# The first two weight units of a decoder layer worked on side by side, their weights in three pieces each

## The reference

```python
def _half_ffn(x, norm_g, w_gate, w_up, w_down):
    h = _rmsnorm(x, norm_g)
    return x + 0.5 * ((jax.nn.silu(h @ w_gate) * (h @ w_up)) @ w_down)

xp = _half_ffn(xp, ffn1_norm, ffn1_w_gate, ffn1_w_up, ffn1_w_down)     # D_FF = 2816
u, q, k, v = _project(_rmsnorm(xp, mix_norm), pos_p, w_in, q_norm, k_norm)
mixed = concatenate([_pool_mix(u, ...), _swa_prompt(q, k, v, sinks)])
xp = xp + mixed @ w_out
xp = _half_ffn(xp, ffn2_norm, ffn2_w_gate, ffn2_w_up, ffn2_w_down)
```

## Time and profile before

| | us |
|---|---|
| median of three runs | 880.23 |
| lowest and highest of them | 879.80, 883.03 |
| the profiled execution, whole | 880.45 |
| its span (first to last instruction) | 878.4 |
| TensorE busy in the span | 871.3 |
| VectorE, ScalarE busy | 660.3, 394.0 |

### The profile page before, as it was taken

How to read it: one execution, slowest core, us unless ns; L and a number is a source line. 1 busy time by engine, 2 the same in 40 slices (tenths; PEclk the granted TensorE clock), 3 DMA queues, 4 the chain that set the end, 5 groups by cost and what they waited for, 6 DMA issues and landing times.

```text
span 878.4 us, 17072 instructions
## 1 busy us (share of the span) xinstructions
PE 871.3 (99%) x7088; PEld 856.9 (98%) x7088; DVE 660.3 (75%) x979; ACT 394.0 (45%) x639; POOL 32.4 (4%) x37
## 2 busy tenths in 40 slices
PE   8999999999999999999999999999999999999998
PEld 7999999999999999999888999999999999999998
DVE  6979647997569986754887697996479975799754
ACT  7635313554224553443754465554125542255420
POOL 0000000000000000012423000000000000000000
PEclk9999999999999999999999999999999999999999
DMA  7333323332424322522321415324233324334241
GB/s 251 117 121 114 133 66 121 121 121 84 145 65 164 121 76 84 190 76 60 113 65 60 145 38 169 120 76 175 75 121 120 121 85 145 111 122 128 85 121 61
DMA packets 43180, 98.57 MB, mean 112 GB/s; under 512 B 4288, under 2 KB 5056, under 8 KB 43104
## 3 DMA queue, kind: packets, MB, share of 16 engines
q1 hardware_dynamic: 41376, 95.01, 33.6%
q10 hardware_dynamic: 1728, 2.48, 0.8%
HBM read 93.53 MB, written 3.60 MB: 111 GB/s over the span
## 4 chain that ended last, share of the span: by engine, by line
PE 96%; DVE 2%; DMA 1%; issue 1%; ACT 0%; SPq 0%; DVEq 0%; ACTq 0%
PE ps L612 44%; PE ps L740 15%; PE ps L742 15%; PE ps L741 15%; PE ps L642 1%; PE ps L978 1%; PE ps L969 1%; DMA xT<-x 1%; PE ps L960 1%; PE ps L799 1%; PE ps L933 0%; PE ps L883 0%; PE ps L657 0%; DVE wlo L1522 0%; DVE hlo L1649 0%
## 5 line engine op out<-in xcount | busy, mean ns | idle before, releaser
L740 PE MATMUL ps<-xhi,whi 128*128 128x260 f32 (+1 forms) x1092 | 310.2, 284 | 0.1
L742 PE MATMUL ps<-xhi,wlo 128*128 128x260 f32 (+1 forms) x1092 | 310.0, 284 | 0.0
L741 PE MATMUL ps<-xlo,whi 128*128 128x260 f32 (+1 forms) x1092 | 309.6, 284 | 0.0
L740 PEld LDWEIGHTS ps<-xhi,whi 128*128 128x128 f32 x1092 | 205.4, 188 | 0.8 <-issue 0.6
L742 PEld LDWEIGHTS ps<-xhi,wlo 128*128 128x128 f32 x1092 | 205.5, 188 | 0.0
L741 PEld LDWEIGHTS ps<-xlo,whi 128*128 128x128 f32 x1092 | 205.4, 188 | 0.0
L1593 DVE TENSOR_TENSOR wlo<-full,whi 128x1024 fp32r<-128x1024 f32 (+1 forms) x117 | 160.3, 1394 | 0.0
L1118 ACT CAST whi<-raw 128x1024 fp32r<-128x1024 f32 (+1 forms) x75 | 75.2, 1003 | 154.9 <-PE ps L612 147.9
L612 PE MATMUL ps<-hhi,whi 128*128 128x268 f32 (+1 forms) x690 | 140.4, 285 | 0.3
L612 PE MATMUL ps<-hlo,whi 128*128 128x268 f32 (+1 forms) x690 | 140.1, 284 | 0.0
L612 PE MATMUL ps<-hhi,wlo 128*128 128x268 f32 (+1 forms) x690 | 139.8, 284 | 0.0
(11 more groups left out here) (194 smaller groups left out, 1070.4 us busy)
## 6 DMA issues: line engine op xcount, KB each, us to landing
full<-gu SPq DMA_DIRECT2D x78, 512.0 KB, 4.4
raw<-d SPq DMA_DIRECT2D x32, 448.0 KB, 3.5
full<-gu SPq DMA_DIRECT2D x39, 256.0 KB, 2.7
raw<-d SPq DMA_DIRECT2D x16, 512.0 KB, 3.7
raw<-w_in SPq DMA_DIRECT2D x10, 512.0 KB, 3.7
raw<-gu SPq DMA_DIRECT2D x9, 512.0 KB, 4.3
raw<-w_out SPq DMA_DIRECT2D x8, 512.0 KB, 4.3
xT<-x SPq DMA_DIRECT2D x8, 268.0 KB, 5.8
```

The source lines that it names most:

```text
L740: nc.tensor.matmul(dst, whi_t, xhi_t, start=(first and pr == 0), stop=False, skip_group_check=True)
L741: nc.tensor.matmul(dst, whi_t, xlo_t, start=False, stop=False, skip_group_check=True)
L742: last = nc.tensor.matmul(dst, wlo_t, xhi_t, start=False, stop=(pr == KC - 1), skip_group_check=True)
```

## The change

- `WARM` goes from 6 to 5.
- The weights of units 0 and 1 come in three pieces each, `PIECES` = tiles 0 and 1, tiles 2 and 3, tiles 4 to 7. `BEFORE_X` gives ahead of which chunk of x (by its place in `ORDER`) a piece is loaded and split: piece 0 of unit 0 ahead of the first chunk, piece 0 of unit 1 ahead of the second, piece 1 of both ahead of the third, piece 2 of both ahead of the fifth. SP, ScalarE and VectorE all follow it.
- TensorE works both units in one loop over the chunks, `first_two`: for each chunk, x high with `whi` and `wlo` of unit 0 and of unit 1, and then x low of the chunk before with `whi` of both. The number of matmuls is the same. `unit_done` is counted up for unit 0 and for unit 1 at the last step.
- `whi_ready` and `wlo_ready` are counted up at the third piece of a unit; the first two pieces have `first_hi` and `first_lo`.
- What follows unit 1 on each engine is as before.

```diff
--- before.py
+++ after.py
@@ -110,8 +110,10 @@
 
 NORM_AT = (1, 2, 6)
 SQSUM_AT = (0, KD - 1, 2 * (KD - 1))
-WARM = 6
-FIRST = 2
+WARM = 5
+PIECES = ((0, 2), (2, 4), (4, 8))
+
+BEFORE_X = {0: ((0, 0),), 1: ((1, 0),), 2: ((0, 1), (1, 1)), 4: ((0, 2), (1, 2))}
 ORDER = (0, 2, 4, 6, 1, 3, 5, 7)
 
 
@@ -295,7 +297,7 @@
     x_loaded = [sem(f"x_loaded{k}") for k in range(KD)]
     fixed_loaded = sem("fixed_loaded")
     gains_loaded = sem("gains_loaded")
-    first_loaded = sem("first_loaded")
+    piece_loaded = [[sem(f"piece_loaded{c}{j}") for j in range(2)] for c in range(2)]
     first_hi = sem("first_hi")
     first_lo = sem("first_lo")
     mixin_loaded = sem("mixin_loaded")
@@ -518,14 +520,16 @@
                 if d == 3 and p < 2:
                     load_unit(s, p + 1, 0)
 
-        sp.dma_start(raw[:, 0, 0:FIRST, :].rearrange("p t c -> p (t c)"), a["gu1"][:, 0:FIRST * P]
-                     ).then_inc(first_loaded, 16)
-        for k in ORDER:
+        def load_piece(c, j):
+            lo, hi = PIECES[j]
+            sp.dma_start(raw[:, c, lo:hi, :].rearrange("p t c -> p (t c)"), a["gu1"][:, (c * KD + lo) * P:(c * KD + hi) * P]
+                         ).then_inc(raw_loaded[c] if j == 2 else piece_loaded[c][j], 16)
+
+        for t, k in enumerate(ORDER):
+            for c, j in BEFORE_X.get(t, ()):
+                load_piece(c, j)
             sp.dma_start(xT[:, k, :], a["x"][:, k, :]).then_inc(x_loaded[k], 16)
-            if k == ORDER[FIRST - 1]:
-                sp.dma_start(raw[:, 0, FIRST:KD, :].rearrange("p t c -> p (t c)"), a["gu1"][:, FIRST * P:KD * P]
-                             ).then_inc(raw_loaded[0], 16)
-        for u in range(1, 2 * PLAIN[0]):
+        for u in range(2, 2 * PLAIN[0]):
             load_plain(0, u)
             if u == 5:
                 load_unit(0, 0, 0)
@@ -632,18 +636,31 @@
             for _ in range(WARM):
                 nc.tensor.matmul(nsum[:, 0, 0:2 * P], hid[:, 0:P], hid[:, 0:2 * P], start=True, stop=True)
 
-        def early(c, dst, pairs, n, wait, first=False, last=False):
+        def first_two(n):
 
             x = x_split(n)
-            for t, k in enumerate(ORDER):
-                for i, (w, lo) in enumerate(pairs):
-                    wait(t, i)
-                    for h in range(2):
-                        done = nc.tensor.matmul(dst[:, h, 0:n], w[:, c % 2, t, :], x(k, lo, h),
-                                                start=(first and t == 0 and i == 0),
-                                                stop=(last and t == KD - 1 and i == len(pairs) - 1))
-            if last:
-                done.then_inc(unit_done, 1)
+            for t in range(KD + 1):
+                for c in range(2):
+                    if t == KD:
+                        break
+                    if c == 0:
+                        pe.wait_ge(xhi_ready, t + 1)
+                    for i, w in enumerate((whi, wlo)):
+                        if t in (0, 2):
+                            pe.wait_ge(first_lo if i else first_hi, t + c + 1)
+                        elif t == 4:
+                            pe.wait_ge(wlo_ready if i else whi_ready, c + 1)
+                        for h in range(2):
+                            nc.tensor.matmul(pair[c][:, h, 0:n], w[:, c, t, :], x(ORDER[t], 0, h),
+                                             start=(t == 0 and i == 0), stop=False)
+                if t:
+                    pe.wait_ge(xlo_ready, t)
+                    for c in range(2):
+                        for h in range(2):
+                            done = nc.tensor.matmul(pair[c][:, h, 0:n], whi[:, c, t - 1, :], x(ORDER[t - 1], 1, h),
+                                                    start=False, stop=(t == KD))
+                        if t == KD:
+                            done.then_inc(unit_done, 1)
 
         def norm_sums(i, c0, n):
 
@@ -668,33 +685,11 @@
...
             warm_up()
-            early(0, pair[0], [(whi, 0), (wlo, 0)], n, hi_there, first=True)
-            early(0, pair[0], [(whi, 1)], n, lo_there, last=True)
-            early(1, pair[1], [(whi, 0), (whi, 1)], n, hi_1, first=True)
-            early(1, pair[1], [(wlo, 0)], n, lo_1, last=True)
+            first_two(n)
             plain(2, turn, [0, 1])
             norm_sums(0, 0, n)
             plain(2, turn, [2, 3])
@@ -1305,16 +1300,20 @@
 
         act.wait_ge(consts_made, 2)
         nc.scalar.copy(warm[:, :], eps[:, :]).then_inc(warmed, 1)
-        act.wait_ge(first_loaded, 16)
-        nc.scalar.copy(whi[:, 0, 0:FIRST, :], raw[:, 0, 0:FIRST, :]).then_inc(first_hi, 1)
-        act.wait_ge(gains_loaded, 16)
-        for k in ORDER:
+
+        def piece_hi(c, j):
+
+            lo, hi = PIECES[j]
+            act.wait_ge(raw_loaded[c] if j == 2 else piece_loaded[c][j], 16)
+            nc.scalar.copy(whi[:, c, lo:hi, :], raw[:, c, lo:hi, :]).then_inc(whi_ready if j == 2 else first_hi, 1)
+
+        for t, k in enumerate(ORDER):
+            for c, j in BEFORE_X.get(t, ()):
+                piece_hi(c, j)
+            if t == 0:
+                act.wait_ge(gains_loaded, 16)
             act.wait_ge(x_loaded[k], 16)
             x_hi(x_pair(xhi7, k, NH_ALL), k, 0, 0, NH_ALL)
-            if k == ORDER[FIRST - 1]:
-                act.wait_ge(raw_loaded[0], 16)
-                nc.scalar.copy(whi[:, 0, FIRST:KD, :], raw[:, 0, FIRST:KD, :]).then_inc(whi_ready, 1)
-        split_hi(1)
         for k in range(KD):
             nc.scalar.activation(sqx[:, k, :], xT[:, k, :], ACT.Square).then_inc(sqx_ready, 1)
             if k == 3:
@@ -1762,22 +1761,22 @@
                     if d:
                         add_square(1, d, 0, NH_ALL)
 
-        def first_weights_lo(hi_there, tiles):
-
-            dve.wait_ge(hi_there, 1)
-            return nc.vector.tensor_tensor(wlo[:, 0, tiles, :], raw[:, 0, tiles, :], whi[:, 0, tiles, :].bitcast(F32),
-                                           ALU.subtract)
-
-        first_weights_lo(first_hi, slice(0, FIRST)).then_inc(first_lo, 1)
-        dve.wait_ge(gains_loaded, 16)
+        def piece_lo(c, j):
+
+            lo, hi = PIECES[j]
+            dve.wait_ge(whi_ready if j == 2 else first_hi, c + 1 if j == 2 else 2 * j + c + 1)
+            nc.vector.tensor_tensor(wlo[:, c, lo:hi, :], raw[:, c, lo:hi, :], whi[:, c, lo:hi, :].bitcast(F32),
+                                    ALU.subtract).then_inc(wlo_ready if j == 2 else first_lo, 1)
+
         for t, k in enumerate(ORDER):
+            for c, j in BEFORE_X.get(t, ()):
+                piece_lo(c, j)
+            if t == 0:
+                dve.wait_ge(gains_loaded, 16)
             x_lo(x_pair(xlo7, k, NH_ALL), x_pair(xhi7, k, NH_ALL), t, k, 0, 0, NH_ALL)
-            if t == FIRST - 1:
-                first_weights_lo(whi_ready, slice(FIRST, KD)).then_inc(wlo_ready, 1)
         dve.wait_ge(fixed_loaded, 16)
         nc.vector.tensor_scalar(nsink[:, :], fixed[:, C_SINK:C_IDENT], -1.0, None, ALU.mult)
         nc.vector.tensor_scalar(ngain[:, :], gains[:, 0:3 * KD], -1.0, None, ALU.mult).then_inc(ngain_made, 1)
-        split_lo(1)
 
         for k in range(1, KD):
             dve.wait_ge(sqx_ready, k + 1)
```

More of the change, by code:

```diff
@@ L669, in plain_products_1 @@
             n = NH_ALL
[L671 to L688, removed]
             def plain(c, dst, ks=None):
```

## The result

| | before | changed |
|---|---|---|
| median of the executions timed side by side, us | 882.9 | 887.69 |
| lowest and highest of them | 879.8, 883.49 | 886.19, 889.27 |
| profiled execution, whole and span | 880.45, 878.4 | 886.19, 884.1 |
| its mean granted clock | 1.000 | 0.994 |

The ratio is 1.0065, 95% interval 1.005 to 1.008: slower by 0.65%, 4.8 us between the two medians, where 0.26% was forecast as the likeliest and 885.2 was the upper end of the range. The two profiled executions are 5.7 us of span apart.

What follows compares the result with a forecast made beforehand. TensorE was taken as the bound, 96% of the span; the profiled 880.45 plus 2.3 us of lag gave 882.75, and 882.6 with the median 0.2 lower. The range was 880.6 to 885.2.

Steps and rivals of the forecast that it cites:

- The supply and E: Opening, units 0 and 1: chunks and casts keep up, TensorE waits last for the third chunk until 8.8, finishing at 18.2.
- E: Time at which TensorE finishes the first two units: 18.2 us, floor 17.4, 19.1 with slow small pieces.
- The release of unit 0's place: Unit 2's cast must wait until unit 0 is finished; TensorE idles 3.6 us and resumes at 21.8, 1.05 later than before.
- lag: How much later TensorE runs than in the kernel before: 2.3 us at the spread, kept to the end; 1.5 to 3.2.
- The clock: TensorE's granted clock in the new 3.6 us hole: the forecast counted no fall to half pace.
- a rival with 0.18 of the chance: TensorE's clock falls in the new hole, half pace from 21.8 to 27.1: lag 3.4 to 4.5, 884.0 to 884.9; chance 0.18.
- Matmuls close on both sides: Reason for giving the clock's fall less chance: the long hole has matmuls close before and after it.
- the 5.3 us of the start: Work TensorE needed at kernel start before reaching the upper clock level, taken as the length of half pace behind the hole.
- The base: Starting time of the sum: profiled execution 880.45 us, median of three runs 880.23.
- the same: Forecast outcome, on the slow side: 0.26% slower, under the 0.5% a measurement can tell from no change; chance 0.87.

Runs made afterwards that it cites:

- e1: Changed kernel with a place of its own for unit 2's high and low parts, so their making waits for no unit: 881.55 us, ratio to before 0.9997.
- e2: Kernel before with one edit, the cast of unit 2 waits until both first units are finished: 889.72 us, ratio 1.0096.
- e3: Changed kernel with 28 matmuls into an unused bank between the first two units and unit 2, filling TensorE's hole: 885.37 us, ratio to before 1.0036.
- f2: Changed kernel with all eight squares ahead of unit 2's cast and all sums ahead of its low part: 886.71 us, ratio to before 1.0067.
- f3: Changed kernel with unit 2's parts in their own place, made before the squares; sums of x and norm later: 883.69 us, ratio to before 1.0025.
- f1: Changed kernel again without an edit, for its spread and a second profile: 885.55 us, ratio to before 1.0049.
- g2: Changed kernel once more without an edit, for a third profile of its opening: 887.23 us, ratio to before 1.0062.
- e4: Kernel before with 21 matmuls into an unused bank behind unit 1, delaying what follows without an added wait: 884.63 us, ratio 1.0034.

## Why the prediction was wrong

By its steps:

- *The supply and E* held: E = 18.2 forecast, 18.5 measured. The third chunk came earlier than in the earlier trace rows (7.42 instead of 8.03), but the fifth, behind the last 512 KB of pieces, is cast only at 11.20, and TensorE takes it up at 12.00, 0.4 later than the matmuls ahead would have let it; the 52 matmuls from there at 0.1236 end at 18.4. That step named the third chunk as the last wait, and it is the fifth.
- *The release of unit 0's place* held, and is the cause: e1 takes it away and nothing is lost, e2 puts it in alone and more is lost. Cast 18.3 forecast, 18.51 measured; unit 2 at 21.8 and 22.05; spread at 27.15 and 27.50; lag 2.3 and 2.64. Of the 2.64 the waits make 2.35 (e3) and the clock 0.3. The lag stayed to the end.
- *The clock* is the step that failed. The sum put it at nothing and left it to a rival with 0.18 of the chance; it fell in the hole or right behind it in all three profiles of the changed kernel, and in e2, f2 and f3. "Matmuls close on both sides" was no reason: e2, f1, f2 and g2 have them too. The rival's size was 3.4 to 4.5 of lag with half pace for 5.3 us, taken from the start. Measured, half pace is either about 3.4 us long (lag 2.64, cheaper than forecast, because the sums were late anyway) or about 10 (lag 5.25, dearer: the second 12 matmuls and the spread are at half pace too). Nor is the 5.3 us of the start a fixed length: in the changed kernel's first profile the first pair, at 5.35, is at the upper level already, 4.2 us after the start of work, and in the third (g2) the matmuls are only from about 7 on. On the mean the fall costs 1.9 (e3). The Trainium skill, "TensorE: Matmul & The Clock Gate", Part 1, had said that a hole lets the clock fall; the traces agree, 0.50 behind 3.4 us of idle time. The same part of the Trainium skill says that activity brings the upper level back. That fits the first profile better than the third, where half pace goes on for 9 us of busy TensorE.
- *The base* failed too. The sum stood on one profiled execution of 880.45 and a median of three of 880.23, and so put half pace in the middle part at nothing. Of 56 executions the mean is 881.6: 40 have some of it. The profile read had none, and one of the three times, 883.03, is by its size one that had two stretches; it was taken for scatter, and the range went down for it instead of up. This shifted the predicted time by 1.4, and is no effect of the change.

Together: 881.6 + 2.35 (waits) + 1.9 (clock in the hole) = 885.8, and the mean of 15 executions is 886.8. The missing 1.0 is already in e3, whose mean of 884.9 lies that much above 881.6 + 2.35, while its groups lie only 0.1 to 0.3 above before and the waits: five of its nine executions are at 0.996. e4's mean is 0.3 above its shift. So it would be more half pace in the middle part; with so few executions that is argued, not shown, and whether the change has a share in it stays open. The forecast "the same" fell with the clock: the waits alone (2.4 to 2.7 by e3's groups) would have stayed under the 4.4 us, 0.5%, that the prediction set between no change and one. The rival's own 884.0 to 884.9 fell short of 886.8 as well, by the base and by the openings with 10 us of half pace. The part of the prediction on the waits came true by its steps and not by luck: e1, e2 and e3 each show them.

## What to carry to other kernels

Working on two units side by side frees both of their places at the end: look for who waits to overwrite the first, and for what is queued behind that wait on its engine, before counting the holes that are filled. Ask of each new hole of TensorE what it does to the granted clock (the shortest that half pace followed here was 1.5 us, with ten small matmuls behind it), and count both outcomes: half pace for the matmuls right behind it, or for all of the next 10 us. A hole that is made shorter may give nothing back: f3's of 1.5 us cost half pace for 6.8. And compare times by the mean granted clock of each execution before reading 3 us into a difference of medians; a base of three executions can lie a whole group off.

## What the runs showed of the hardware

- Half-pace stretches also arise where TensorE has no hole of over 0.8 us. In the middle part each costs 1.5 us in the profiles and 1.4 to 1.6 between groups, and the same program has none, one or two of them from one execution to the next (880.1, 881.7, 883.2); one profile (e4) has a stretch of twice the length instead. Ahead of one TensorE was thinly used (0.55 busy at 426), but so it was in the kernel before (0.38 at 424), whose clock stayed up. What sets them off stays open.
- A hole of 3.3 to 3.6 us was followed by 0.50 in all five profiles that had one (changed three times, e2, f2); one of 1.5 us with ten small matmuls behind it was too (f3); holes of 0.9 and 0.5 (e1), 0.5 (e3) and 1.25 were not.
- How long half pace lasts behind the same hole differs: about 3.4 us in two profiles of the changed kernel, about 10 in the third and in e2 and f2; behind f3's hole it was 6.8. What decides it stays open.
- Sums that each wait for the one ahead on VectorE stand 0.8 apart (5.64 us for seven in f2, 2.36 for three in the earlier trace rows), where the instruction behind a sum that doesn't wait for it starts after 0.63.
